# Two transformer blocks on one core: output product by row tiles, the second memory projection moved into later waits, the down bias added behind the expert loop

## The reference, cut to what matters

```python
mix = merged @ w_out[l]
x = x + gt_m * rms_norm(mix, mix_post_g[l])
h2 = rms_norm(x, ffn_pre_g[l]) * (1.0 + sc_f) + sh_f
logits = h @ router_w + router_b
top_val, top_idx = lax.top_k(logits, 4)      # of 32 experts
top_w = softmax(top_val)
...                                          # each expert: gate, up, SwiGLU
act @ w_down[e] + b_down[e]                  # weighted by top_w and summed
...
x = x + gt_f * rms_norm(ff, ffn_post_g[l])
```

## Time and profile before

| what | value |
|---|---|
| median of 3 runs | 2384.41 us (2384.03 to 2393.8) |
| the profiled execution | 2387.95 us, of them 2386.2 us span |
| mean granted clock of PE | 0.935 of full |
| PE busy | 2038.5 us, 85% of the span |
| DVE, ACT, POOL busy | 644.3, 411.7, 103.6 us |
| moved from memory | 573.27 MB, 241 GB/s over the span |

### The profile page before, as it was taken

One profiled execution on the slowest core, in us unless ns is written; L12 is line 12 of the kernel. 1 busy time (PEld: TensorE's weight loads), 2 busy tenths in 40 slices (PEclk: granted clock), 3 DMA queues, 4 the chain that ended last, 5 costly groups with the idle time before them and its releaser, 6 DMA issues.

```text
span 2386.2 us, 25533 instructions
## 1 busy us (share of the span) xinstructions
PE 2038.5 (85%) x10223; PEld 1169.8 (49%) x10224; DVE 644.3 (27%) x1194; ACT 411.7 (17%) x600; POOL 103.6 (4%) x116
## 2 busy tenths in 40 slices
PE   6989897999997878997977887999989487769998
PEld 4645462333332222332322744887477486738863
DVE  5655232212111111221111333100055545430001
ACT  2211122211112111121122211100022221120000
POOL 2000200000000000000000100200000122100000
PEclk9999988999999989999988998999999698889999
DMA  9555459998999999989999721443433000023420
GB/s 326 197 212 195 159 205 428 428 420 318 428 427 428 428 427 428 400 341 427 428 428 418 264 104 59 127 143 141 157 121 129 35 1 1 1 81 123 159 88 18
DMA packets 106325, 575.37 MB, mean 241 GB/s; under 512 B 7255, under 2 KB 8787, under 8 KB 81648
## 3 DMA queue, kind: packets, MB, share of 16 engines
q1 hardware_dynamic: 102000, 563.46, 59.2%
q0 software_dynamic: 4256, 10.92, 1.6%
HBM read 573.27 MB, written 1.07 MB: 241 GB/s over the span
## 4 chain that ended last, share of the span: by engine, by line
PE 74%; DMA 14%; DVE 7%; ACT 3%; issue 1%; DVEq 0%; SPq 0%; ACTq 0%
DMA ring<-in_w_up 13%; PE ps L1915 13%; PE ps L1414 10%; PE ps L1926 6%; PE ps L711 6%; PE ps L719 5%; PE ps L1455 4%; PE ps L1428 3%; PE ps L897 2%; PE ps L1476 2%; PE ps L1438 2%; PE ps L2253 2%; PE ps L2259 1%; PE ps L1022 1%; PE ps L2263 1%
## 5 line engine op out<-in xcount | busy, mean ns | idle before, releaser
L1915 PE MATMUL ps<-arena,ring 128*128 128x256 f32 x1408 | 304.4, 379 | 1.8 <-issue 1.8
L1915 PEld LDWEIGHTS ps<-arena,ring 128*128 128x128 f32 x1408 | 267.4, 190 | 38.4 <-issue 2.1
L1414 PE MATMUL ps<-ring,arena 128*64 128x512 f32 x1088 | 240.5, 595 | 0.0
L1455 PE MATMUL ps<-ring,arena 128*32 128x512 f32 x1088 | 148.5, 694 | 65.8 <-DMA ring<-in_w_up 65.6
L1926 PE MATMUL ps<-ring,arena 128*128 128x512 f32 x352 | 151.4, 592 | 0.0
L1414 PEld LDWEIGHTS ps<-ring,arena 128*64 128x64 f32 x1088 | 75.3, 137 | 152.4 <-issue 152.4
L711 PE MATMUL ps<-arena,ring 128*128 128x256 f32 x608 | 132.8, 380 | 0.0
L1428 PE MATMUL ps<-ring,arena 128*64 128x512 f32 x544 | 120.5, 594 | 12.5 <-ACT arena L1377 12.5
L711 PEld LDWEIGHTS ps<-arena,ring 128*128 128x128 f32 x608 | 115.0, 190 | 16.8 <-issue 1.5
L1455 PEld LDWEIGHTS ps<-ring,arena 128*32 128x32 f32 x1088 | 38.2, 125 | 161.6 <-issue 150.3
L719 PE MATMUL ps<-ring,arena 128*128 128x512 f32 x256 | 113.0, 601 | 3.5 <-ACT arena L2352 2.0
(11 more groups left out here) (535 smaller groups left out, 2286.9 us busy)
## 6 DMA issues: line engine op xcount, KB each, us to landing
ring<-in_w_gate SPq DMA_DIRECT2D x64, 2048.0 KB, 18.6
ring<-in_w_up SPq DMA_DIRECT2D x64, 2048.0 KB, 22.1
ring<-in_w_down SPq DMA_DIRECT2D x64, 2048.0 KB, 19.0
ring<-in_ffn_w_gate_up SPq DMA_DIRECT2D x22, 2048.0 KB, 7.9
ring<-in_ada_w SPq DMA_DIRECT2D x12, 2048.0 KB, 11.2
ring<-in_ffn_w_down SPq DMA_DIRECT2D x10, 2048.0 KB, 7.9
ring<-in_w_in SPq DMA_DIRECT2D x8, 2048.0 KB, 21.6
ring<-in_dn_w_in SPq DMA_DIRECT2D x6, 2048.0 KB, 7.7
```

What stands on the lines that cost most here:

```text
L1414: m = pe.matmul(bank(b)[c * CAP:(c + 1) * CAP, :], xT[:, j * P + h * CAP:j * P + (h + 1) * CAP], w[h][:, j, c * 512:(c + 1) * 512], start= ...
L1455: m = pe.matmul(bank(0)[(2 * i + c) * FEW:(2 * i + c + 1) * FEW, :], XT[:, j * P + h * CAP:j * P + h * CAP + FEW], w[h][:, j, c * 512:(c + ...
L1915: m = pe.matmul(bank(b0 + g)[:, c * SEQ:(c + 1) * SEQ], w[:, k, (2 * g + c) * P:(2 * g + c + 1) * P], hT2[:, k, :], start=(k == 0), stop=( ...
```

## The change

The output product is computed by row tile: tile 0 of the first half, tile 1 of the first half, then tile 0 of the second half, the modulation rows, tile 1 of the second half. `act_s5` and `dve_s5` take each row tile on its own through both norms up to h2. `pe_kv` is split: `pe_mem_keys` for one of two key halves, `pe_mem_values` for one row tile of values. For memory 0 the pieces lie around the turning of h2, the router and the counts. Memory 1 goes behind the expert loop: its keys ahead of `pe_over`, its values between the scores and the probabilities of stage 9, and its weight is loaded behind the last expert's. So the ring has one piece less ahead of the experts. The masks are told apart from the weights (`mk_ready` 1 and 2), DVE computes positions ahead of weights, and the weights are turned last, just ahead of the loop. Banks 4 to 7 are zeroed by DVE, and the down biases are added behind the last expert. POOL loads the gains of stage 9 only when the values of memory 1 are there. Addresses and semaphore counts change to suit.

```diff
-        pc_out = [piece(by_k(A["w_out"][0], n * 512, n * 512 + 512), out_ps, 5 + n + 1) for n in range(2)]
-        pc_mem = [piece(by_k(A["mem_w_kv_2"][i], 0, 2 * MW), mkv_ps, i + 1) for i in range(2)]
+        pc_out = [piece(by_k(A["w_out"][0], n * 512, n * 512 + 512), out_ps, (6, 8)[n]) for n in range(2)]
+        def mem_piece(i):
+            return piece(by_k(A["mem_w_kv_2"][i], 0, 2 * MW), mkv_ps, 2 * i + 2)
+
+        pc_mem = [mem_piece(0)]
...
-            pe_rows(pe, arrived(pe, pc_out[0]), (4, 6), mgT, KD, out_ps)
+
+            def out_rows(n, t):
+                w = arrived(pe, pc_out[n])
+                for k in range(KD):
+                    m = pe.matmul(bank(4 + 2 * t + n), mgT[:, k, t * P:(t + 1) * P], w[:, k, :], start=(k == 0), stop=(k == KD - 1))
+                if n or t:
+                    m.then_inc(out_ps, 1)
+            mod_rows(range(4))
+            out_rows(0, 0)
+            out_rows(0, 1)
+            pe.wait_ge(mod_read, 7)
             pe_turn(pe, mem_nat, "memory")
+            out_rows(1, 0)
             pe_after_turn(pe, "memory")
-            mod_rows(range(4))
-            pe_rows(pe, arrived(pe, pc_out[1]), (5, 7), mgT, KD, out_ps)
-            pe.wait_ge(mod_read, 7)
             mod_rows(range(4, 8))
+            out_rows(1, 1)
             pe.wait_ge(mod_read, 8)
-            pe_kv(pe, 0)
...
-            dve_rms(dve, o, 3)
-            for t in range(TT):
+            for t in range(TT):
+                mean_of(dve, o, ssq, rms, t, 3 + 2 * t)
                 o(dve.scalar_tensor_tensor(mtmp, bank(4 + 2 * t, 2), rms[:, t:t + 1], GTm, ALU.mult, ALU.mult))
                 o(dve.tensor_tensor(x3[:, t, :], x3[:, t, :], mtmp, ALU.add), x1_ready)
+                mean_of(dve, o, ssq2, rms2, t, 4 + 2 * t)
+                o(dve.scalar_tensor_tensor(h2[:, t, :], x3[:, t, :], rms2[:, t:t + 1], Af, ALU.mult, ALU.mult))
+                o(dve.tensor_tensor(h2[:, t, :], h2[:, t, :], Bf, ALU.add), nat_ready)
+
+        def mean_of(dve, o, total, root, t, n):
+            dve.wait_ge(sq_done, n)
+            o(dve.tensor_scalar(root[:, t:t + 1], total[:, t:t + 1], 1.0 / D, EPS, ALU.mult, ALU.add), ms_done)
+            dve.wait_ge(rt_done, n)
+            o(dve.reciprocal(root[:, t:t + 1], root[:, t:t + 1]))
...
+            pe_mem_keys(pe, 0, 2, 0)
+            turn(0)
+            pe_mem_keys(pe, 0, 2, 1)
+            pe.wait_ge(rout_in, 16 * 5)
+            pe.wait_ge(x1_ready, 2)
+            route(0)
+            turn(1)
+            route(1)
+            pe_mem_values(pe, 0, 3, 0)
             pe.wait_ge(mk_ready, 1)
...
+            pe_mem_values(pe, 0, 3, 1)
+
+        def pe_weights_turned(pe):
+            pe.wait_ge(mk_ready, 2)
+            for t, told in enumerate((extra.x_ps, router_ps)):
+                pe.transpose(bank(0, 1, E)[:, t * P:(t + 1) * P], wt[:, t, 0:E], ident).then_inc(told, 1)
             pe.wait_ge(wT_ready, 1)
-            pe.wait_ge(pos_ready, 1)
             pe.wait_ge(bias_in, 16 * 5)
+
+        def pe_down_bias(pe):
             for t in range(TT):
                 for d in range(2):
                     m = pe.matmul(bank(4 + 2 * t + d), wT[:, t * P:(t + 1) * P], bds[:, d * 512:(d + 1) * 512],
-                                  start=True, stop=False, skip_group_check=True)
+                                  start=False, stop=True, skip_group_check=True)
+                m.then_inc(ff_ps, 1)
...
         def dve_s6(dve, o):
+            o(dve.memset(posm, 0.0))
+            o(dve.memset(wt[:, :, E:E + 1], 0.0))
+            dve.wait_ge(turned, H2_TURNS + 4)
+            o(dve.memset(bank(4, 2), 0.0))
...
+            dve_rows(dve, main, 0, 0)
...
+            o(dve.tensor_copy(cnt, bank(7)[:, 2 * E:3 * E]), pos_ready)
+            o(dve.memset(bank(6, 2), 0.0))
             dve.wait_ge(fn_done, 1)
...
+            pe.wait_ge(mkv_ready, 1)
             pe_gather(pe, main, 1)
+            pe.wait_ge(mkv_ready, 2)
             pe_gatherT(pe, main, 1)
+            pe_weights_turned(pe)
...
+            if q == 0:
+                act.wait_ge(main.e_ready, E)
+                act.wait_ge(mkv_ps, 3)
+                o(act.copy(kvKept[:, 0:512], bank(3)), mkv_ready)
             o(act.activation(dummy, con("ones")[:, 0:1], then))
...
+                    if (q, t, b) == (0, 1, 1):
+                        pe.wait_ge(mkv_ready, 3)
...
-            dve_over(dve, o, 0, 4, (ff_ps, E), (x2_ready, 0), GTf, ar(0, D), 0)
+            dve_over(dve, o, 0, 4, (ff_ps, E + 2), (x2_ready, 0), GTf, ar(0, D), 0)
...
+                pc_mem.append(mem_piece(1))
                 w = A["att_w_in_2"][0]
...
         def pool_s9(pool):
             pool.wait_ge(pos_ready, 1)
-            pool_gain(pool, 0, "norm_mix_post_2", 0)
-            pool_gain(pool, 1, "norm_ffn_post_2", 0)
-            pool.wait_ge(ff_ps, E)
+            pool.wait_ge(ff_ps, E + 2)
...
+            pool.wait_ge(mkv_ps, 4)
+            pool_gain(pool, 0, "norm_mix_post_2", 0)
+            pool_gain(pool, 1, "norm_ffn_post_2", 0)
 
         def pe_s9(pe):
+            pe_down_bias(pe)
+            for c in range(2):
+                pe_mem_keys(pe, 1, 3, c)
             pe_over(pe, 0)
...
             for t in range(TT):
+                pe_mem_values(pe, 1, 5, t)
+            pe.wait_ge(mkv_ready, 5)
+            for t in range(TT):
                 for g in range(3):
```

More of the change, by code:

```diff
@@ L308, in kv_of @@
             return x[:, 0:512].rearrange("p (c s) -> p c s", c=2), x[:, 512:1024].rearrange("p (t n) -> p t n", t=TT)
-        kvM = [ar(4096 + 1024 * i, 1024) for i in range(2)]
+        kvM = ar(4096, 1024)
         mem_g = sm(1136, 2 * KD).rearrange("p (i k) -> p i k", i=2)
@@ L1142, in act_s5 @@
             act_turned(act, o, mem_T[0], "memory")
-            act.wait_ge(out_ps, 7)
-            act_rms(act, o, [bank(4 + 2 * t, 2) for t in range(TT)], ar(10240, D), 3)
+            for t in range(TT):
+                act.wait_ge(out_ps, 7 + t)
+                square_of(act, o, bank(4 + 2 * t, 2), ssq, rms, t, 3 + 2 * t)
+                act.wait_ge(x1_ready, t + 1)
+                square_of(act, o, x3[:, t, :], ssq2, rms2, t, 4 + 2 * t)
         FIRST = len(pieces)
@@ L1216, in pool_s6, with turn, route @@
                     dma(pool, bgu[(2 * i + c) * E:(2 * i + c + 1) * E, :], A[a][0][:, c * 512:(c + 1) * 512], bias_in)
+        H2_BANK = (0, 4)
+        H2_TURNS = turn_base("experts")
         def pe_s6(pe):
[L1219 to L1223, removed]
+            def turn(t):
+                pe.wait_ge(nat_ready, TT * TURNS.index("experts") + t + 1)
+                for b in range(2):
+                    for k in range(4):
+                        kk = 4 * b + k
+                        m = pe.transpose(bank(H2_BANK[t] + b)[:, k * P:(k + 1) * P], h2[:, t, kk * P:(kk + 1) * P], ident)
+                    m.then_inc(turn_ps, 1)
+            def route(t):
+                pe.wait_ge(turned, H2_TURNS + 2 * t + 2)
                 for k in range(KD):
@@ L1246, in pe_s6, with act_weights_turned @@
                     m = pe.matmul(bank(4 + 2 * t + d), wT[:, t * P:(t + 1) * P], bds[:, d * 512:(d + 1) * 512],
[L1247 to L1249 removed]
+                                  start=False, stop=True, skip_group_check=True)
+                m.then_inc(ff_ps, 1)
         def act_s6(act, o):
[L1252 to L1255, removed]
+            for t in range(TT):
+                for b in range(2):
+                    act.wait_ge(turn_ps, H2_TURNS + 2 * t + b + 1)
+                    o(act.copy(h2T[:, 4 * b:4 * b + 4, t * P:(t + 1) * P], bank(H2_BANK[t] + b).rearrange("p (k m) -> p k m", k=4)), turned)
+                if t == 0:
+                    act.wait_ge(mkv_ps, 1)
+                    o(act.copy(kvM[:, 0:512], bank(2)), mkv_ready)
             act.wait_ge(fn_asked, 1)
             o(act.activation(ew, ew, ACT.Exp), fn_done)
[L1258 removed]
+            act.wait_ge(mkv_ps, 2)
+            o(act.copy(kvM[:, 512:1024], bank(3)), mkv_ready)
+        def act_weights_turned(act, o):
             act.wait_ge(router_ps, 4)
@@ L2024, in act_s9 @@
                 o(act.activation(em3[t], em3[t], ACT.Exp), fn_done)
+            act.wait_ge(mkv_ps, 4)
+            o(act.copy(kvKept[:, 512:1024], bank(5)), mkv_ready)
             for n in range(6, 12):
```

104 lines of the change are left out of this document (49 added, 55 removed).

## The result

The changed kernel takes 2373.33 us (median of 7 runs, 2369.99 to 2378.12), the kernel before, run on the same chip, 2387.32 (7 runs, 2384.03 to 2393.8). The ratio is 0.9944, interval 0.9929 to 0.9959. So the change gains 0.56%, about 13 us, where I had forecast 25.8. The direction was right, and the time lies 2.3 us above the range of 2351 to 2371. It stands at the edge of what I called measurable (0.5%). Of the 14.7 us between 2358.6 and 2373.33, 2.9 are the base (2384.41 was the median of the three runs that I started from, 2387.32 is the median with four more); the rest, 11.8, is gain that did not come. The experiments ran beside the kernel before on several chips, so they are best compared by their ratios to it. Times and ratios leave out slow runs, of which there was one, in e4 (3836 us, at a granted clock of 0.734).

A forecast was written before the change was run, and what follows sets the result against it. Loads bound the expert loop (DMA 98% busy) and PE's queue the stretch ahead, so an earlier start ends earlier. -28.0 + 3.5 - 0.5 - 0.8 = -25.8 off the median 2384.41 gives 2358.6 us; range 2351 to 2371.

The forecast's parts named there:

- Part 3: Behind the loop: bias product adds 3.5 us, all on the path; memory 1's keys hidden, with -0.5 up to L1811.
- My upper bound of 5.76: Behind the loop: the most the bias product would take, as before, mostly at half clock; lower bound 1.99.
- 6.92 in the 9.06 us that PE waits for DVE: Behind the loop, ahead of L1811: memory 1's keys fit under PE's wait, with 2.1 us to spare.
- The wait inside `pe_over` for ACT's copy: Behind the loop: a new wait, as bank 3 must be copied by ACT (0.6) behind its four turned copies.
- Parts 1 and 2: Ahead of the loop: row tiles finish the router 14.8 sooner; with memory 1 moved out, experts start 28.0 sooner, at 321.8.
- my lower bound of 24: Ahead of the loop: the least by which the first expert would start sooner; forecast 28.0, upper bound 30.
- rival A: Half clock in the new start, 297 to 320: loop starts at 328, 6 us later, total 2364.8; chance 12%.
- Part 4: Stage 9: memory 1's values (6.92) lie free in the 9.49 us softmax wait; -0.8 from a better clock.
- Rival D: Stage 9: SP's queue held at the attention output weight, its late load making the kernel slower; chance 4%.
- Rival C: Expert loop hands the gain back, bound by a transfer stream begun with expert 0: -7.6, total 2376.8; chance 8%.
- Rival B: Warm clock throughout: start at 319.7, L1811 at full clock, 1.7 in stage 9: -29.9, total 2354.5; chance 9%.
- my list: Signs to check, including three of a wrong prediction: clock 0.50 from 298 on, loop longer than 961, bias over 5.8.

The follow-up runs named there:

- e4: Changed kernel with the down-bias product, still behind the loop, laid on four groups of 32 rows: 2376.1 us, ratio 0.9933.
- e1: Kernel before with one tiny product (128x32) put behind the expert loop, ahead of L1811: 2388.43 us in one run, beside 2388.12 for before.
- e9: The changed kernel itself, run again for its second profile: 2374.53 us, ratio 0.9954.
- e7: Kernel before with only the down biases moved behind the loop and their banks zeroed: 2397.02 us, ratio 1.0036.
- e8: Changed kernel with three unread filler products in PE's two pauses around the router: 2375.2 us, ratio 0.9938.
- e10: Changed kernel with three unread filler products around the router, run once more: 2375.19 us, ratio 0.9942.
- e3: Changed kernel with the down biases back ahead of the loop, opening the sums, without zeroing the banks: 2371.74 us, ratio 0.9926.
- e5: Changed kernel with the biases ahead of the loop and half of memory 1's keys moved to stage 9: 2365.05 us, ratio 0.9891.
- e6: As e5, with the biases ahead of the loop on four groups of 32 rows: 2361.12 us, ratio 0.9874.
- e11: As e6, with three unread filler products around the router: 2359.19 us, ratio 0.9878.
- e2: Changed kernel without any down-bias product, so the term is missing from its result: 2368.29 us, ratio 0.9923.

## Why the prediction was wrong

**The step that failed: Part 3**, "so I take 4 x 0.875 = 3.5, all on the path". It fails twice. *The pause*: I put the bias product right behind the last combine. PE issues nothing for 4.8 us there; e1 shows it in the old kernel too, and it is between 4.78 and 5.05 in all of the changed kernels. *The size*: behind the pause the product took 6.83, 6.88, 6.67, 6.72 and 7.19 in five profiles (the changed kernel, e9, e7, e8, e10), twice the 3.5, with a mean granted clock of 0.50 to 0.54 in it. Ahead of the loop it took 7.19 in e3, at 0.50, and 3.87 in e5, at 0.94: so my 3.5 was near the price at full clock, and what it missed is the clock. My upper bound of 5.76 was too low for a product wholly at half clock (4 x 1.75 = 7.0). That the four go one after another because they share 32 rows was right: on four groups they take 1.14, 1.50 and 1.89 (e6, e11, e4). Together 4.8 + 6.83 - 3.5 = +8.1, less 0.4 for `pe_over` (from DVE's start to the first projection 13.3, where it was 14.2: -0.9, I had -0.5), makes the 7.7 of the table. e7 shows the sign of this part by itself: +8.6. The rest of the gain that did not come lies ahead of the loop in the first profile (4.4 us), and in pieces of 1.4 us and less in the second.

The same oversight stands in "6.92 in the 9.06 us that PE waits for DVE". The cover is 9.06 long, but PE can work only in the last 4.2 of it. With the bias ahead of them the keys hide under a cover that begins later; without it they stick out (e2, where the stretch is 3.7 longer). The wait inside `pe_over` for ACT's copy came to 0.47, small as I had it.

What the pause is: that PE waits for its own next code is the reading which fits the instruction packet in it and e1. A second pause speaks for it. Between the first and the second expert PE stands still as well, and by how much goes with the packet. e8 and e10 are the same program; the first expert product of the second expert in e8, and below it in e10:

```profile
349.62 1.10 PE L1503 MATMUL ps<-arena 128*128 128x512 f32 x2 [0.90 <-issue]
350.74 2.04 PE L1503 MATMUL ps<-arena 128*128 128x512 f32 x2 [5.88 <-issue]
```

In e8 an instruction packet stands 3.1 us ahead of the end of the first expert's combine, in e10 1.7 us behind it. The other profiles with the new order divide in the same way: with the packet 1.6 to 2.0 us behind that end the pause is 5.72 to 6.11 (the changed kernel, e9, e2, e3, e5, e11), with the packet 2.6 to 3.0 us ahead of it 1.41 and 1.09 (e4, e6). Still no run changed where the code lies, so the cause is argued and not shown. The Trainium skill, Runtime: NRT & Kernel Launch, section Instruction fetch mechanics, says that a taken branch to a place outside the instructions held forces a DMA fetch and stalls the engine, while code in a row comes ahead of need. The trace agrees with that rule, which I had not weighed in the prediction, with 4.8 us as the length here; the page gives none.

**Parts 1 and 2: right, within the scatter of the clock.** The stage came out at 66.2 in the second profile, where I had 65.9 (321.8 less 255.9), and at 70.25 in the first, a gain of 23.6 against my lower bound of 24. Of the 4 us between them 2.7 are rival A: the router's second tile 3.62 or 1.97, the first values 6.23 or 5.39. The other 1.3 come ahead of the router, from the spreads and the output product at the start of the stage (2.09 and 16.07, or 1.14 and 15.70), which rival A did not have. I had called A's condition unlikely, as the new pauses are short; behind the pause of 1.90 the clock fell ahead of the router's second tile in one execution, and only in the values in the other. So A's fall is the usual case, in six of seven profiles without fillers, and 12% was too little for it; against e2's stage of 65.6, where the clock held, the stage of the changed kernel is 0.6 to 4.6 us longer in its two profiles, where I had put 6. Of the rule that I cited from the Trainium skill, TensorE: Matmul & The Clock Gate, section HAM oscillation, the trace agrees with the direction: the clock was 1.00 from the router to the first values in the three filled profiles, though e2 had it without fillers. The pieces were near: a pause of 1.90 for 1.8, DVE's zeroing 0.91 for 1.2. That the sum comes so close has luck in it. In the second profile the four quarters of the output product take 29.9 (15.70, 7.03 and 7.13) where I had 28.0, and the first values 5.39 for 3.46; against that, the router was in the sum at 5.74, the time of a product that had run partly at half clock, and takes 1.94 and 1.97. A wait that I did not have is the 2.29 ahead of L1500.

**Part 4: the cover right, its small gain not shown.** The wait is down to 2.43 (2.6 forecast), the values cost nothing, and e5 and e6 put 3.7 us more there for nothing. That the stretch is 0.9 shorter (0.8 forecast) shows nothing by itself: in e7, which leaves stage 9 alone, it is 131.7 where the kernel before has 133.4, and in e8, which has the values there, 133.2. **Rival D** fell: stage 9's output product is not held by its weight. **Rival C** fell: the loop is 961 to 964 us in all, whatever its start. **Rival B** (warm throughout) never came: in every profile with the bias or the keys right behind the pause the clock falls to 0.50 in them.

Against my list: the loop of 961 and stage 9's wait came as named. The product behind DVE's norm (`pe_over`) began 20.5 us behind the last combine, not 12.6. The bias over 5.8 and the clock of 0.50 in the router's stretch are two of the three signs that I had named for a wrong prediction.

## What to carry to other kernels

Idle time of an engine right behind a loop is not all cover: here the first 4.8 us of PE's 9.06 could take no work, and a tiny product of no dependence shows such a pause in one run. Before work is moved behind a loop, put the pause and the half clock behind it into the price, and move only what fits into what is left of the cover; e5 does that, with the bias back ahead of the loop, and turned 0.56% into 1.1%. A product that uses 32 rows takes about a quarter of the time on four groups of rows (e4, e6), though no run time told that gain apart here. And before a remedy is credited with a better clock, look whether the clock was better already ahead of it.

## What the runs showed of the hardware

- PE issues nothing for 4.78 to 5.05 us behind the expert loop, in all 12 profiles in which something was there to issue. A like pause of 5.96 stands between the first and the second expert of the changed kernel (346.81 to 352.77 in the chain of waits), and one of 0.90 or 5.88 in two executions of one program (e8, e10), as its instruction packet comes before or behind the end of the first expert's combine; the loop's length doesn't show it.
- Products behind that pause run at 0.50 for the first microseconds: the bias 6.7 to 7.2 in place of 3.9 (e5, at 0.94), and the keys, partly at 0.50 (0.78 on the mean in the changed kernel), 8.7 to 9.2 in place of 7.1 (the values, of as many columns, take 7.17 in stage 9).
- Four products of 32 rows and 512 columns took 6.7 to 7.2 us on the same 32 rows at a mean clock of 0.50 to 0.54 and 3.87 at 0.94, and 1.1 to 1.9 on four groups of rows.
- Zeroing two banks (128x1024) takes DVE 0.91 us.
- Two executions of one program differed by 4 us in a stage of 70 through the granted clock alone (1.14 or 2.09 for the same eight products at its start).
